# A two-block transformer kernel: the router moved between the out product's tiles, its top-k split in two, a ninth buffer for expert matrices

## What is computed

```python
x = x + merged @ w_out                       # 512 x 1024
h = rms_norm(x, ffn_norm)
g_prob = softmax(h @ w_group + b_group)      # 8 groups
g_w, g_idx = top_k(g_prob, 1)
e_sel = (h @ w_expert + b_expert).reshape(T, 8, 8)[arange(T), g_idx]
top_v, top_i = top_k(e_sel, 2)               # 2 experts of 64 for a token
gate = g_w * softmax(top_v)
# tokens sorted by expert, in blocks; for a block of expert e:
y = (silu(xb @ w1[e]) * (xb @ w3[e])) @ w2[e]
x = x + (gate * y, added back at its token)
```

## Time and profile before

| what | value |
|---|---|
| three runs, us | 2040.62, 2042.19, 2044.79 |
| span of the profiled execution, from its first to its last instruction, us | 2036.1 |
| the time around it, against the median, us | 6.1 |
| TensorE busy | 1766.1 us, 87% |
| VectorE busy | 902.1 us, 44% |
| ScalarE busy | 738.8 us, 36% |
| POOL busy | 265.5 us, 13% |
| mean granted TensorE clock | 0.963 |
| DMA | 506.17 MB, mean 249 GB/s |
| matrices of experts by SyncE | 192 of 2048 KB |

### The profile page before, as it was taken

One profiled execution on the slowest core, in us unless ns is written; L12 is line 12 of the kernel. 1 busy time (PEld: TensorE's weight loads), 2 busy tenths in 40 slices (PEclk: granted clock), 3 DMA queues, 4 the chain that ended last, 5 costly groups with the idle time before them and its releaser, 6 DMA issues.

```text
span 2036.1 us, 37869 instructions
## 1 busy us (share of the span) xinstructions
PE 1766.1 (87%) x15190; PEld 1275.6 (63%) x15190; DVE 902.1 (44%) x1699; ACT 738.8 (36%) x1382; POOL 265.5 (13%) x281
## 2 busy tenths in 40 slices
PE   7999999787877777787778777779989999999998
PEld 5677788644444444444444444458867799998877
DVE  5555335532222222232222223266265698886245
ACT  4444522233222322222232222252365554445143
POOL 0000000000000000000000000640010078880000
PEclk9999999899998998998999889999999999999999
DMA  6222222799999999999999999944230233333322
GB/s 209 79 84 69 78 102 91 309 371 421 427 425 427 426 426 427 426 426 426 427 425 427 426 427 426 421 144 113 79 95 1 73 94 115 108 109 117 102 83 83
DMA packets 109058, 506.17 MB, mean 249 GB/s; under 512 B 9480, under 2 KB 59016, under 8 KB 75696
## 3 DMA queue, kind: packets, MB, share of 16 engines
q1 hardware_dynamic: 100864, 492.07, 60.6%
q10 hardware_dynamic: 6512, 8.94, 1.7%
q0 software_dynamic: 1600, 4.02, 0.8%
HBM read 497.32 MB, written 2.11 MB: 245 GB/s over the span
## 4 chain that ended last, share of the span: by engine, by line
PE 59%; DMA 29%; DVE 6%; ACT 2%; issue 2%; SPq 1%; POOL 0%; ACTq 0%; DVEq 0%
DMA ring<-in_w 28%; PE bank L686 13%; PE bank L687 12%; PE bank L688 12%; PE bank L2572 8%; PE bank L2484 4%; PE bank L2563 3%; PE bank L874 2%; PE bank L900 1%; PE bank L886 1%; DVE w_lo L791 1%; SPq L2115 1%; PE bank L2581 1%; DMA raw<-in_w_in 1%; ACT w_hi L775 1%
## 5 line engine op out<-in xcount | busy, mean ns | idle before, releaser
L2572 PE MATMUL bank<-ring,XTs 128*32 128x256 f32 x4032 | 284.0, 424 | 107.9 <-DMA ring<-in_w 107.1
L2827 DVE TENSOR_TENSOR x<-x,bank 128x512 f32<-128x512 f32 x264 | 163.8, 681 | 477.1 <-PE bank L2563 476.3
L2572 PEld LDWEIGHTS bank<-ring,XTs 128*32 128x32 f32 x4032 | 154.1, 119 | 238.9 <-issue 175.8
L2581 PE MATMUL bank<-ring,aT 128*32 128x256 f32 x2048 | 123.8, 381 | 90.2 <-DVE aT L2847 90.2
L2351 ACT ACTIVATE y<-bank 32x256 f32<-32x256 f32 x256 | 95.9, 375 | 225.4 <-PE bank L2563 139.0
L686 PE MATMUL bank<-hTh,w_hi 128*128 128x512 f32 x362 | 146.4, 404 | 5.8 <-DVE hTl L838 4.4
L791 DVE TENSOR_TENSOR w_lo<-raw,w_hi 128x2048 fp32r<-128x2048 f32 (+4 forms) x47 | 96.5, 2058 | 122.0 <-ACT w_hi L775 121.8
L2484 PE MATMUL bank<-arena,oh 128*32 128x256 f32 x2048 | 145.3, 422 | 4.4 <-DVE oh L2809 1.1
L2581 PEld LDWEIGHTS bank<-ring,aT 128*32 128x32 f32 x2048 | 66.5, 109 | 128.8 <-issue 96.4
L687 PE MATMUL bank<-hTh,w_lo 128*128 128x512 f32 x362 | 142.5, 394 | 0.0
L688 PE MATMUL bank<-hTl,w_hi 128*128 128x512 f32 x362 | 142.5, 394 | 0.0
(11 more groups left out here) (467 smaller groups left out, 3691.2 us busy)
## 6 DMA issues: line engine op xcount, KB each, us to landing
ring<-in_w SPq DMA_DIRECT2D x190, 2048.0 KB, 19.5
raw<-in_w_in SPq DMA_DIRECT2D x25, 1024.0 KB, 5.5
late_raw<-in_w_gate SPq DMA_DIRECT2D x11, 1024.0 KB, 5.4
late_raw<-in_w_up SPq DMA_DIRECT2D x11, 1024.0 KB, 5.3
late_raw<-in_w_down SPq DMA_DIRECT2D x11, 1024.0 KB, 5.0
raw<-in_w_out SPq DMA_DIRECT2D x4, 1024.0 KB, 5.0
third<-in_w SPq DMA_DIRECT2D x2, 2048.0 KB, 17.4
raw<-in_w_o SPq DMA_DIRECT2D x4, 1024.0 KB, 5.2
```

Of the source, the lines that this page charges most:

```text
L2572: mm = pe.matmul(Hb[BLK * j:BLK * (j + 1), :], XTs[u][:, 4 * (c % 2) + 2 * h + c // 2, :], w[:, at_:at_ + Q], start=(h == 0 and c == 0), s ...
L2581: mm = pe.matmul(Yb[BLK * j:BLK * (j + 1), :], aT[:, r, h, :], ring[3 * u + 2][:, at_:at_ + Q], start=(h == 0 and r == 0), stop=(h == 1 an ...
L2827: ins = v.tensor_tensor(xs, xs, Sb[t % 2][n][:, :], ALU.add)
```

## The change

- The router reads the raw rows of `x`, not the normed ones: `ffn_norm` is multiplied into its weights `w_r` (new VectorE instruction behind a wait for the six loads), and each tile's 1/rms is applied to the logits. A tile's two column halves are turned and multiplied apart (`rows_turned(i, n)`, `router(i, n)`, four matmuls each), and `between` puts these on TensorE behind the tiles of `out1`. Their banks are those of `out0`.
- `dve_top` runs the top-k for tiles 0 and 1, and again for tiles 2 and 3; the add of the last tile stands between them. Instructions for each tile become one for two tiles in three places.
- The normed rows `h2` are made by POOL (`x_gained`, `x` times gain) and ScalarE (times 1/rms) in place of VectorE's L2782.
- The four rank products go into one bank; the first selection `oh` follows right behind them on VectorE, and the first `gather` stands before `starts` on TensorE.
- SyncE: w1 of expert 2 is asked for when the merged rows are split, two matrices when the first part of `out1` is used, two more at its end; w2 of expert 2 has a buffer of its own, `ninth`, in three pieces, asked for when `tab` is complete. w2 of expert 4 then follows at `w_used` 4.
- The parts of split weights and of `hT` lie interleaved, so that buffers come free singly. Three late loads share one semaphore, as do two early signals.

```diff
+        hT_all = at("hT_all", F0 + 8192, [2, 2, 4, T], F32R)
...
-        w_hi = at("w_hi", W0 + RAW * UNIT, [PARTS, UNIT], F32R)
-        w_lo = at("w_lo", W0 + (RAW + PARTS) * UNIT, [PARTS, UNIT], F32R)
+        w_split = at("w_split", W0 + RAW * UNIT, [PARTS, 2, UNIT], F32R)
...
+        ninth = [at("ninth_a", F0 + 5120, [5, 512]), at("ninth_b", F0 + 45056, [3, 512])]
...
+            return w_split[:, (u.n + 1) % PARTS, 0, 0:n] if u.late is None else late_hi[:, u.late % 2, 0:n]
...
-        plan("hT2", DC)
-        plan("router", NT)
-
-        plan("rank", NT, among=(1, 2, 3, 4))
+        J["hT2"] = bk.take(2 * NT, [job.bank for job in J["out0"][0:2]])
+        J["router"] = bk.take(2, [job.bank for job in J["out0"][2:4]])
+
...
+                    if after:
+                        after(k, j)
...
+        xT = [[at(f"xT{n}{k}", F0 + 28672 + 1024 * n + 512 * k, [4, P])[:, :, :] for k in range(2)] for n in range(2)]
+        x_gained = [scratch[:, 1472:1472 + D], at("x_gained", F0 + 30720, [D])[:, :]]
...
+        def dve_logits(v, chain, pair):
+            job = J["router"][pair[0] // 2]
+            full(v, job)
+            for i in pair:
+                lo = NR * 2 * (i % 2)
+                half = [banks[job.bank][:, lo + NR * n:lo + NR * (n + 1)] for n in range(2)]
+                ins = v.scalar_tensor_tensor(logit[:, i, :], half[0], rstd[:, i:i + 1], r_row, ALU.mult, ALU.add)
+            chain(ins)
...
+            chain(v.tensor_tensor(gsel[:, some, :], iota8.rearrange("p (o g) -> p o g", o=1).broadcast_to([P, n, NG]),
+                                  gidx4[:, some, :].broadcast_to([P, n, NG]), ALU.is_equal))
...
+            job = J["rank"][0]
+            full(v, job)
+            free(v.scalar_tensor_tensor(by_tile[:, 0:NT, :], banks[job.bank][:, 0:NT * NE].rearrange("p (i n) -> p i n", i=NT),
+                                        1.0, both, ALU.add, ALU.mult), job)
+            read(v, [job])
+
+            v.tensor_tensor(oh[0][:, :, :], tab[:, 0, 0:NT].rearrange("p (t o) -> p t o", o=1).broadcast_to([P, NT, BLK]),
+                            places[:, 0:1, :].broadcast_to([P, NT, BLK]), ALU.is_equal).then_inc(made_oh, 1)
...
-            v.tensor_tensor(oh[0][:, :, :], tab[:, 0, 0:NT].rearrange("p (t o) -> p t o", o=1).broadcast_to([P, NT, BLK]),
-                            places[:, 0:1, :].broadcast_to([P, NT, BLK]), ALU.is_equal).then_inc(made_oh, 1)
...
+            sp.wait_ge(S("merged_lo"), DC)
+            load_matrix(0, 0, 2, third[0], S("third"))
             sp.wait_ge(lo_made, order[n_first - 1].count)
             load_matrix(0, 0, 0)
+            used(sp, units_of["out1"][0])
+            load_matrix(0, 1, 0)
+            load_matrix(1, 0, 1)
             full(sp, order[n_first - 1].last)
-            for u, m in ((0, 1), (0, 2), (1, 0), (1, 1)):
-                load_matrix(u, m, u)
-
-            full(sp, J["router"][-1])
+            load_matrix(0, 2, 0)
+            load_matrix(1, 1, 1)
+            full(sp, J["router"][1])
             sp.wait_ge(S("h2"), NT)
-            for m in range(2):
-                load_matrix(0, m, 2, third[m], S("third"))
+            load_matrix(0, 1, 2, third[1], S("third"))
+            sp.wait_ge(S("tab"), 1)
+            src = weights[2][2:3].rearrange("a (h p r) n -> p (a h) (r n)", h=2, p=P)
+            sp.dma_start(ninth[0][:, 0:4, :].rearrange("p k n -> p (k n)"), src[:, 0, :]).then_inc(S("ninth"), 16)
+            sp.dma_start(ninth[0][:, 4, :], src[:, 1, 0:512]).then_inc(S("ninth"), 16)
+            sp.dma_start(ninth[1][:, :, :].rearrange("p k n -> p (k n)"), src[:, 1, 512:2 * D]).then_inc(S("ninth"), 16)
...
-            load_matrix(0, 2, 2)
+            load_matrix(0, 2, 4)
...
-            sp.wait_ge(w_used, 2 * STEPS + 4)
-            load_matrix(0, 2, 4)
...
+                if i >= 2:
+                    act.wait_ge(S("routed"), (2 if n else 0) + i - 1 + (2 if n else 0))
+                free(act.activation(xT[n][i % 2], by_chunk(job), ACT.Copy), job)
+            def squares(i):
                 read(act, [J["out0"][i], J["out1"][i]])
-                n2.act(act, i, x[:, i, :], av(12288, D), ssq, rstd)
-                if i:
-                    turned(i - 1)
-            turned(NT - 1)
+                n2.act_squares(act, i, x[:, i, :], h2[:, i, :], ssq)
+
+            def rows_gained(i):
+                act.wait_ge(S("r2"), 2 * (i // 2) + 2)
+                act.wait_ge(S("x_gained"), i + 1)
+                act.activation(h2[:, i, :].rearrange("q (c p) -> q c p", c=DC), by_eighths(x_gained[i % 2]), ACT.Copy,
+                               scale=rstd[:, i:i + 1]).then_inc(S("h2"), 1)
+
+            turned(0, 0)
+            turned(1, 0)
+            turned(2, 0)
+            squares(0)
+            turned(3, 0)
+            n2.act_root(act, 0, rstd)
+            turned(0, 1)
+            turned(1, 1)
+            squares(1)
+            n2.act_root(act, 1, rstd)
+            squares(2)
+            turned(2, 1)
+            rows_gained(0)
+            rows_gained(1)
+            squares(3)
+            n2.act_root(act, 2, rstd)
+            n2.act_root(act, 3, rstd)
+            rows_gained(2)
+            rows_gained(3)
...
+            def rows_turned(i, n):
+
+                job = J["hT2"][NT * n + i]
+                read(pe, J[f"out{n}"][i:i + 1])
+                claim(pe, job)
+                for c in range(4):
+                    lo = P * (4 * n + c)
+                    mm = pe.transpose(banks[job.bank][:, P * c:P * (c + 1)], x[:, i, lo:lo + P], ident)
+                fill(mm, job)
+
+            def router(i, n):
+
+                job, lo = J["router"][i // 2], NR * (2 * (i % 2) + n)
+                if n == 0 and i == 0:
+                    pe.wait_ge(S("rank_consts"), 3)
+                if n == 0 and i % 2 == 0:
+                    claim(pe, job)
+                read(pe, J["hT2"][NT * n + i:NT * n + i + 1])
+                for c in range(4):
+                    mm = pe.matmul(banks[job.bank][:, lo:lo + NR], xT[n][i % 2][:, c, :], w_r[:, 4 * n + c, :],
+                                   start=(c == 0), stop=(c == 3))
+                if n and i % 2:
+                    fill(mm, job)
+                else:
+                    mm.then_inc(S("routed"), 1)
+
+            def between(k, j):
+
+                if k == 0 and j:
+                    rows_turned(j - 1, 0)
+                    if j > 1:
+                        router(j - 2, 0)
+                elif k and j == 0:
+                    router(2, 0)
+                    rows_turned(3, 0)
+                elif k and j == 1:
+                    router(3, 0)
+                    rows_turned(0, 1)
+                    rows_turned(1, 1)
+                    router(0, 1)
+                elif k:
+                    router(j - 1, 1)
+                    rows_turned(j, 1)
+
             for n in range(2):
-                pe_token(pe, f"out{n}", hT, wait=lambda k: pe.wait_ge(S("merged_lo"), 4 * (k + 1)))
-
-            def gather(u):
+                pe_token(pe, f"out{n}", hT, wait=lambda k: pe.wait_ge(S("merged_lo"), 4 * (k + 1)), after=between if n else None)
+            router(3, 1)
...
+            pe.wait_ge(made_oh, 1)
+            gather(0, first=True)
 
             job = J["starts"][0]
...
+            def added(i, n):
+                job, xs = J[f"out{n}"][i], x[:, i, 512 * n:512 * (n + 1)]
                 full(v, job)
-                free(v.tensor_copy(h2T[:, 4:8, P * i:P * (i + 1)], by_chunk(job)), job)
-
-            for n in range(2):
-                ahead(lo_until, v, f"out{n}")
-                for i, job in enumerate(J[f"out{n}"]):
-                    full(v, job)
-                    xs = x[:, i, 512 * n:512 * (n + 1)]
-                    ins = v.tensor_tensor(xs, xs, banks[job.bank][:, :], ALU.add)
-                    free(ins, job)
-                    if n:
-                        rows_normed(i - 1)
-            rows_normed(NT - 1)
-            turned(NT - 1)
+                free(v.tensor_tensor(xs, xs, banks[job.bank][:, :], ALU.add), job)
+
+            ahead(lo_until, v, "out0")
+            v.wait_ge(S("w_r"), 96)
+            gains = prm[:, slice(*PARAM_COLS["ffn"])].rearrange("p (c o) -> p c o", o=1)
+            v.tensor_tensor(w_r, w_r, gains.broadcast_to([P, DC, NR]), ALU.mult).then_inc(S("rank_consts"), 1)
+            for i in range(NT):
+                added(i, 0)
+            ahead(lo_until, v, "out1")
+            added(0, 1)
+            added(1, 1)
+            n2.dve(v, chain, 0, ssq, rstd)
+            added(2, 1)
+            n2.dve(v, chain, 1, ssq, rstd)
+            v.sem_inc(S("r2"), 2)
+            dve_logits(v, chain, (0, 1))
+            dve_top(v, chain, slice(0, 2))
+            added(3, 1)
+            n2.dve_mean(v, 2, ssq, rstd)
+            job = J["hT2"][2 * NT - 1]
+            full(v, job)
+            full(v, J["router"][0])
+            free(v.tensor_copy(xT[1][1], by_chunk(job)), job)
```

(12 more changed lines are left out.)

217 lines of the change are left out of this document (98 added, 119 removed).

## The result

The changed kernel takes 2053.1 us (median of 4, 2052.5 to 2055.4) against 2041.4 us: a ratio of 1.0059, interval 1.0046 to 1.0072. It is slower, as forecast, but by 11.7 us in place of 6.6 and just outside the range.

A forecast was written before the change was run, and what follows sets the result against it. The prediction took the kernel's end as a fixed distance behind `w_used` 14, set by TensorE's walk. `both` 3.8 us later plus 2.8 us longer to the second gather gave 6.6: 2042.2 + 6.6 = 2048.8 us, range 2038 to 2053.

The forecast's parts named there:

- Anchor: Matrix stream: the kernel's end stands at a fixed distance, 871 us, from `w_used` 14, which TensorE's walk sets.
- Loads worth nothing: First pairs: ninth buffer and earlier loads gain nothing, since nobody in the walk waits for a matrix.
- The rival that prefetch counts: First pairs held by matrices, not TensorE: up to 6.9 us gained, some 2036 to 2038; chance 0.18.
- Step 1: Out product's end, until the last `out1` tile is full: 12.9 us later.
- a group of four is about 0.46: 13 x 0.46 = 6.0: Seven turn and six router groups inserted ahead of the last `out1` tile's end: 6.0 us.
- the 0.95: TensorE's two waits for a just finished tile, at tiles 0 and 2, in `out1`: 0.45 and 0.5 us.
- The stall: TensorE stands still behind `out1`'s second tile, as VectorE's add waits behind `w_r`: 4.25 us (3.0 to 4.9).
- the clock: TensorE's granted clock falls after that idle time in `out1`, costing 1.7 us (0 to 3.4).
- Step 2: From the last `out1` tile full to `both` complete: 9.2 us shorter, so `both` comes 3.8 us later.
- turn 0.55, copy 0.7, router 0.55: Tile 3's times in us between its add and its logits, behind the first top-k batch.
- Step 3: From `both` to the second gather: 2.8 us longer, as `starts` waits for the first gather's end.
- a rival with 0.09: Clock stays at 0.5 through `hidden` (up to +2), POOL's fourth `x_gained` late (+1): about 2052; chance 0.09.

The follow-up runs named there:

- e15: The six edits of e14 on the changed kernel, but with the loads of the kernel before (no ninth buffer): 2044.0 us, ratio 1.0017.
- e14: Changed kernel with `w_r` wait behind out0's adds, tile 3's add/copy inside top-k, `starts` inside gather, second selection and further copy earlier, third `x_gained` buffer: 2040.3 us.
- e6: Changed kernel with the whole SyncE part undone (loads of the kernel before, no ninth buffer): 2052.8 us, ratio 1.0054.
- e3: Changed kernel with the two `starts` products moved back ahead of the first gather: 2048.9 us, ratio 1.0038.

## Why the prediction was right and wrong

**Anchor: right.** The end kept its distance from `w_used` 14 in the changed kernel and all experiments but e15. In all of them it is 1.2 to 2.5 us longer than in the kernel before (883.8 to 885.0 against 882.6), with new loads and with old; why was not tried and stays open. The parts of the change that I had given slack (layout, joined semaphores) were not varied singly; e14 has them all and costs nothing against the kernel before.

**Loads worth nothing: right for this kernel** (e6), for the reason given. The rival that prefetch counts falls here, but e14 against e15 shows its mechanism, and sooner than I had put it ("`both` over 7 us before 395"): e14 has `both` only 1.2 us earlier than the kernel before. The old loads are asked for at the out product's end, and that now lies 9 us later; I had left this out of the rival's condition.

**Step 1: the term "a group of four is about 0.46: 13 x 0.46 = 6.0" failed**: with the 0.95 beside it 9.0 was measured, since a router product is two records and a group of four takes 0.8 to 1.0. The stall was 3.4 (forecast 4.25), the clock 2.7 (forecast 1.7; 0.2 to 2.5 in other profiles). That these two nearly cancel is luck.

**Step 2: right in kind, 2.7 us short.** POOL blocked VectorE as said, 2.0 in the row and 2.4 to 2.6 when taken away (forecast 1.6, bound 2.5). What failed is "turn 0.55, copy 0.7, router 0.55": behind an idle of 3.86 us the turn and the router product took 1.12 and 1.98, at half the clock, and the router product alone takes 1.0 at the full clock. From the add's end to the logits it was 4.0 us, forecast 1.8. I had seen the low clock for the gather and not for what stands ahead of it.

**Step 3: the sentence "starts `hidden` at 9.5 and ends it at 13.0: no longer what decides, unless its clock stays low" failed in its second half.** `hidden` started at 9.8 and ended near 15.8, since its clock was low; at the full clock it would have ended at some 13.2, ahead of the selection (13.6). I gave this to a rival with 0.09, and it was what happened. That the start was so near is partly luck: TensorE claims bank 7 ahead of `hidden`, and L1524, which frees it, stands behind VectorE's whole gate chain, a wait of 2.12 us that I had not seen; the gather and `starts` ahead of it took 0.8 us less than forecast. "`starts` waits for its end" was the right place, priced at 2.8 and worth 4.0 with the clock (e3).

## What to carry to other kernels

Before costing a matmul group from a profile, divide its records by the products in the code: here a router, gather or expert product in float32 is two records; a turn, or a product of the split parts in the out product, is one. Follow every claim of a bank (the wait of TensorE until the bank's last reader is through) to the instruction that frees it, and ask what that one stands behind after the change. And price TensorE's idle times twice, once for the wait and once for what runs behind it: where several short waits follow one another, moving two products that take half a microsecond moved the next stretch by four, half of it by the clock, and such a share has to be a range: it differed between profiles with equal waits.
